# Down-projections of a two-layer kernel: four direct products against seven products of half-size blocks, with block sums made by accumulating DMAs in DRAM

## Reference

```python
FFN_DIM = 2816                      # 22 blocks of 128

def conv_ffn(h, w_up, w_dw, b_dw, w_down):
    u = depthwise_conv(h @ w_up, w_dw) + b_dw      # h (1, 1024, 1024), w_up (1024, 5632), width 3
    gate, val = jnp.split(u, 2, axis=-1)
    return (jax.nn.silu(gate) * val) @ w_down      # (1024, 2816) @ (2816, 1024)

# in each layer, after the token mixer:
h = modulate(rmsnorm(x_lat, g_pre_ffn[i]), m_lat[3], m_lat[4])
x_lat = x_lat + m_lat[5] * rmsnorm(conv_ffn(h, ...), g_post_ffn[i])
```

## Time and profile before

| | us |
|---|---|
| median of 3 runs | 2531.25 (2530.59 to 2535.36) |
| span of the profiled execution, first to last instruction | 2526.5 |
| PE busy in it | 2466.9 (98%) |
| DVE, ACT, POOL busy | 1870.6, 1237.6, 916.5 |

### The profile page before, as it was taken

The page is one execution under the profiler, slowest core; times in us unless marked ns, Lnnn a source line. Parts: engine busy times, 40 slices in busy tenths (PEclk is TensorE's granted clock), DMA queues, the critical chain, the costliest instruction groups (busy, mean ns, idle before and its releaser), DMA issues.

```text
span 2526.5 us, 31835 instructions
## 1 busy us (share of the span) xinstructions
PE 2466.9 (98%) x11292; PEld 1989.2 (79%) x11292; DVE 1870.6 (74%) x2445; ACT 1237.6 (49%) x1998; POOL 916.5 (36%) x611
## 2 busy tenths in 40 slices
PE   8989999999899999999999999999999999999998
PEld 3878888888688788888888877757887888888886
DVE  4467676767458999999437379997689999994352
ACT  3356665666444555555435342236545555554331
POOL 0067486861044566653002100000445656630001
PEclk9999999999999999999999999999999999999999
DMA  6033243330521222222635321020212222236361
GB/s 265 27 109 113 84 133 100 125 100 26 196 100 59 84 88 81 83 88 96 229 130 175 113 80 34 34 67 34 100 59 84 85 82 84 83 101 225 125 207 69
DMA packets 102000, 262.48 MB, mean 104 GB/s; under 512 B 11104, under 2 KB 12384, under 8 KB 101856
## 3 DMA queue, kind: packets, MB, share of 16 engines
q1 hardware_dynamic: 88752, 213.85, 24.8%
q0 software_dynamic: 11520, 41.95, 5.2%
q10 hardware_dynamic: 1584, 4.85, 0.6%
HBM read 216.56 MB, written 44.04 MB: 103 GB/s over the span
## 4 chain that ended last, share of the span: by engine, by line
PE 79%; DVE 15%; issue 2%; ACT 1%; DMA 1%; POOL 0%; SPq 0%; DVEq 0%; POOLq 0%; ACTq 0%
PE psum L2146 23%; PE psum L2148 23%; PE psum L2147 23%; DVE acts L2056 3%; DVE acts L2058 3%; PE psum L2362 3%; PE psum L2351 1%; PE psum L2352 1%; DVE weights_f32r L1753 1%; DVE acts L2060 1%; DVE small L1655 1%; PE psum L2179 1%; DMA low<-x_t 1%; DVE high_f32r L1874 1%; PE psum L2447 1%
## 5 line engine op out<-in xcount | busy, mean ns | idle before, releaser
L2146 PE MATMUL psum<-acts_f32r,weights_f32r 128*128 128x512 f32 x1728 | 683.8, 396 | 8.6 <-DVE acts_f32r L1520 3.0
L2148 PE MATMUL psum<-acts_f32r,weights_f32r 128*128 128x512 f32 x1728 | 674.1, 390 | 0.0
L2147 PE MATMUL psum<-acts_f32r,weights_f32r 128*128 128x512 f32 x1728 | 673.8, 390 | 0.0
L803 POOL TENSOR_TENSOR low<-low 128x512 f32<-128x512 f32 x91 | 132.1, 1452 | 965.4 <-ACT low L1125 960.5
L886 ACT ACTIVATE weights_f32r<-low 128x512 fp32r<-128x512 f32 (+2 forms) x501 | 325.3, 659 | 319.4 <-PE psum L2148 244.5
L2146 PEld LDWEIGHTS psum<-acts_f32r,weights_f32r 128*128 128x128 f32 x1728 | 325.3, 188 | 79.8 <-issue 5.6
L1886 DVE TENSOR_TENSOR weights_f32r<-low,weights_f32r 128x512 fp32r<-128x512 f32 x264 | 379.5, 1482 | 0.1
L2148 PEld LDWEIGHTS psum<-acts_f32r,weights_f32r 128*128 128x128 f32 x1728 | 325.0, 188 | 68.8
L2147 PEld LDWEIGHTS psum<-acts_f32r,weights_f32r 128*128 128x128 f32 x1728 | 325.3, 188 | 68.2 <-issue 2.4
L1893 DVE TENSOR_TENSOR weights_f32r<-low,weights_f32r 128x512 fp32r<-128x512 f32 x176 | 125.6, 719 | 233.9 <-ACT weights_f32r L886 231.0
L830 POOL TENSOR_TENSOR low<-low 128x512 f32<-128x512 f32 x150 | 265.7, 1772 | 39.8 <-DVE acts_f32r L1871 29.3
(11 more groups left out here) (248 smaller groups left out, 4665.7 us busy)
## 6 DMA issues: line engine op xcount, KB each, us to landing
low<-units SPq DMA_DIRECT2D x130, 512.0 KB, 4.0
low<-units SPq DMA_DIRECT2D x176, 256.0 KB, 3.4
set<-mod_w POOLq DMA_DIRECT2D x80, 512.0 KB, 3.9
gated<-low SPq DMA_DIRECT2D x44, 512.0 KB, 2.6
low<-gated SPq DMA_DIRECT2D x88, 256.0 KB, 3.9
residual<-low SPq DMA_DIRECT2D x48, 256.0 KB, 2.0
acts<-mod_w SPq DMA_DIRECT2D x4, 1024.0 KB, 8.8
low<-x_t SPq DMA_DIRECT2D x4, 1024.0 KB, 17.7
```

The lines of the kernel that those rows point to most:

```text
L803: pool.tensor_tensor(acc, first, ring(n), ADD).then_inc(sq_added, 1)
L2146: pe.matmul(out, wl, xh, start=first, stop=False, skip_group_check=continued)
L2147: pe.matmul(out, wh, xl, start=False, stop=False, skip_group_check=continued)
L2148: return pe.matmul(out, wh, xh, start=False, stop=last, skip_group_check=continued)
```

## The change

The contraction of 22 blocks is cut in two halves of 11 (KB), the output in two halves and the tokens in two halves, and the 2 x 2 block product is made as seven products t = 0 to 6 of 11 steps each (ITEMS = 77 steps of 12 matmuls for each layer, before 88). The sums of weight blocks ("S") and of gated blocks ("T") that they need are built in DRAM by DMAs issued by POOL, some of them accumulating; negated gated half blocks, which those sums need, are made by a new ACT copy (`negated`) and stored by SP. Four of the seven results are not an output alone, and DVE combines them (`down_part`). Each step now loads and splits a weight and a gated half block of its own.

```diff
+KB = FB // 2
+ITEMS = 7 * KB
+DOWN = (("W", 0, "B", 0), ("W", 1, "G", 0), ("S", 1, "T", 2), ("S", 0, "T", 4), ("W", 2, "T", 3), ("S", 3, "T", 1), ("S", 2, "G", 1))
+DOWN_BANKS = (0, 0, 1, 0, 1, 0, 0)
 def dn_slot(i):
-    return (i + 2) % 6
+    return (i + 2) % 8
 # SP
             def store_g(layer, j):
                 sp.wait_ge(g_new, FB * layer + j + 1)
+                g = f((FIRST_T if j < 3 else MAIN_T) + L)
+                if j < KB:
+                    dst, g = t_d[layer][j, 0:4].rearrange("i p n -> p i n"), g[:, 0:HALF].unsqueeze(1).to_broadcast([P, 4, HALF])
+            def store_negated(layer, j):
+                sp.wait_ge(n_new, FB * layer + j + 1)
+                sp.dma_start(t_d[layer][j, 4] if j < KB else n_d[layer][j - KB], f(NEGATED, HALF)).then_inc(n_out, 16)
...
 # POOL
+            def weight_sum(layer, n):
+                m, part = divmod(n, 4)
+                sums, base = s_d[layer][m].rearrange("i p n -> p i n"), U_FFN[layer] + 2 * FB + m
+                wait(pool, summed, weights_summed(layer, n))
+                if part == 0:
+                    pool.dma_start(sums, units[base][:, HALF:L].unsqueeze(1).to_broadcast([P, 4, HALF])).then_inc(summed, 16)
+                if part == 1:
+                    pool.dma_start(sums[:, 0:3], units[base][:, 0:HALF].unsqueeze(1).to_broadcast([P, 3, HALF]),
+                                   accum_op=ADD, max_dma_last_dim=4 * HALF).then_inc(summed, 16)
...
                     if k + 2 < CB:
                         pool.dma_start(part, modw[t + 2, k + 2]).then_inc(mod_in[k % 2], 16)
+                    for n in range(4 * KB * (t * CB + k) // (10 * CB), 4 * KB * (t * CB + k + 1) // (10 * CB)):
+                        weight_sum(0, n)
+            def gated_sum(layer, j):
+                pool.wait_ge(g_out, 16 * (FB * layer + j + 1))
+                pool.wait_ge(n_out, 16 * (FB * layer + j + 1))
+                at, n = max(j - KB, 0), j if j < KB else 2 * j - KB
+                sums = t_d[layer][j % KB].rearrange("i p n -> p i n")
+                pool.wait_ge(summed, gated_summed(layer, n))
+                if j < KB:
+                    pool.dma_start(sums[:, 1:4], t_d[layer][j, 4].unsqueeze(1).to_broadcast([P, 3, HALF]), accum_op=ADD, max_dma_last_dim=4 * HALF).then_inc(summed, 16)
+                else:
+                    pool.dma_start(sums[:, 2:5], g_d[layer][at][:, HALF:L].unsqueeze(1).to_broadcast([P, 3, HALF]),
+                                   accum_op=ADD, max_dma_last_dim=4 * HALF).then_inc(summed, 16)
+                    pool.wait_ge(summed, gated_summed(layer, n + 1))
+                    pool.dma_start(sums[:, 3], n_d[layer][at], accum_op=ADD, max_dma_last_dim=4 * HALF).then_inc(summed, 16)
...
                     pool.tensor_tensor(f(U_V + HALF, HALF), f(S_7, HALF), f(S_5, HALF), ADD).then_inc(c22_new, 1)
+                    gated_sum(layer, p)
+                for j in range(MAIN, FB):
+                    gated_sum(layer, j)
...
             down(1)
+            for n in range(4 * KB):
+                weight_sum(1, n)
             mixer(2)
 # ACT, in the up-projection
                         act.wait_ge(c22_new, m)
+                        negated(p + 1)
                         mid(p + 2, 1, f(U_V))
 # DVE, in the down-projection
+                for i in range(6, ITEMS + 4):
+                    t, j = divmod(i, KB)
+                    if i < ITEMS:
+                        split(i)
+                    if t == 7 and j == 0 and b == 1:
+                        t_start(b, 0)
+                        for k in range(CB + 2):
+                            if k < CB:
+                                t_block(b, 0, k)
+                            if k >= 2:
+                                t_rest(b, 0, k - 2, next_h, C_MOD + MODS)
...
+                    if 63 <= i < 70:
+                        renewed(i - 63)
+                    if j == 3 and t:
+                        for c in range(4):
+                            down_part(t - 1, c)
+                    if (t, j) == (5, 7):
+                        stat_scale()
+                        renew_start(b, 0)
+                    if (t, j) == (6, 3):
+                        renewed(7)
 # PE, ahead of the first matmuls of product t into the bank of output block c (bank_free)
+                    if t == 6:
+                        pe.wait_ge(part_new, 24 * layer + 16 + c + 1)
 # PE, in product t
+                    if (t, step) == (5, 2):
+                        pe.wait_ge(part_new, 24 * layer + 16)
+                        stat_cols(b, 0, "y")
+                    if (t, step) == (5, 4):
+                        stat_spread(RT_POST)
```

More of the change, by code:

```diff
@@ L665, in ffn @@
                     load_up(layer, v)
-                for j in range(2):
-                    store_g(layer, j)
+                store_g(layer, 0)
+                store_negated(layer, 0)
+                store_g(layer, 1)
                 for p in range(MAIN):
@@ new lines, in ffn @@
+                for i in range(4, ITEMS):
+                    t, j = divmod(i, KB)
+                    load_down(layer, i)
+                    if i == 6:
+                        store_negated(layer, FB - 2)
+                    if i == 7:
+                        store_g(layer, FB - 1)
+                    if i == 9:
+                        store_negated(layer, FB - 1)
+                    if t == 1 and j == 4:
+                        sp.wait_ge(mm_done, op_done(layer, MAIN - 1, 6))
+                        sp.wait_ge(x_out, 16 * 16 * b)
+                        load_residual(b, 0)
+                    if t == 6 and 1 <= j < 9:
+                        store_x(b, 0, j - 1)
@@ L1225, in silu, with negated @@
                     act.activation(f(at), f(at), ACT.Silu).then_inc(silu_g, 1)
+                def negated(j):
+                    at = (FIRST_T if j < 3 else MAIN_T) + L + (HALF if j < KB else 0)
+                    act.wait_ge(g_new, j0 + j + 1)
+                    wait(act, n_out, 16 * (j0 + j))
+                    copy(f(NEGATED, HALF), f(at, HALF), -1.0).then_inc(n_new, 1)
                 def combined(t, k):
@@ L2589, in ffn, with down @@
                         group_done(mm)
-                def down(turn, j, c):
-                    i = FB * turn + j
+                def down(t, j, c):
+                    i = KB * t + j
                     if c == 0:
                         pe.wait_ge(w_lo, w0 + 139 + i + 1)
-                        if turn % 2 == 0:
-                            pe.wait_ge(g_lo, 2 * FB * layer + FB * (turn // 2) + j + 1)
-                    return three(bank(2 * c + turn % 2), half_unit(dn_slot(i))[c], [g_at(j, p) for p in range(2)], j == 0, j == FB - 1)
@@ L2632, in ffn @@
                     for c in range(4):
-                        for j in range(FB - 4, FB):
-                            mm = down(turn, j, c)
-                            if c == 3 or j == FB - 1:
+                        for j in range(KB - 4, KB):
+                            mm = down(t, j, c)
+                            if c == 3 or j == KB - 1:
                                 group_done(mm)
```

434 lines of the change are left out of this document (224 added, 210 removed).

## The result

The changed kernel takes **2650.4 us** (median of 4 runs, 2646.2 to 2653.3) against 2530.9 us for the kernel before beside it (4 runs, 2526.5 to 2535.4): ratio 1.0467, 95% interval 1.0446 to 1.0489. It is 4.7% slower. Predicted were 2504 us and a range of 2482 to 2588; the prediction is wrong in sign and range.

A forecast was written before the change was run, and what follows sets the result against it. PE, busy 98% of the span, was taken as the bound. Terms -59.8 + 16.4 + 2 + 8.2 + 5.0 + 0.8 = -27.4 us took the span from 2526.5 to 2499.1; plus 4.75 to the median, 2504 us, range 2482 to 2588.

The forecast's parts named there:

- What goes: Matmul steps of 12 fall from 88 to 77 in each of two layers, removing 59.8 us of PE's work.
- POOL in the up-projection: In pairs 11 to 16 POOL's wait for an accumulating DMA overruns its free time: 8.2 us a layer, +16.4 us.
- L: Landing time of an accumulating DMA POOL waits for in pairs 11 to 18, taken as 6.4 us, bounds 3.9 and 8.8.
- 6G - 36.2: Up-projection cost in us a layer over six rounds, G being POOL's new DMA work, L + 1.0, taken as 7.4.
- Attention: 44 weight-sum DMAs hide in POOL's 20 us free per three vectors; loads queued behind sums cost +2 us.
- The upper bound, 66: Attention's largest cost, 66 us, if each weight sum costs POOL 4 us.
- Module: In layer 1's convolution module 44 sums at 5.9 us each take 260 us, hidden in a 300 us gap: 0.
- The threshold of 6.8 us: In the convolution module the sums stay hidden while their mean time stays under 6.8 us.
- Product 6: PE waits 4.1 us a layer at product 6's start for DVE to read product 5's banks: +8.2 us.
- End of layer 0: DVE's scaling, combinations and first unit split finish after PE ends the last product: +5.0 us, bounds 1 and 9.
- Loads: In the down-projection 22 loads of 256 KB a product, 193 GB/s, four steps in flight, cost nothing.
- slow accumulation: Rival, chance 0.28: accumulating DMAs land in 9 us, closing POOL's gaps in up-projection, attention and module: 2585 us; at 12, well over 2650.

The follow-up runs named there:

- e4: Changed kernel with all accumulating DMAs writing without adding, so both sums are left out; number, shapes, order and waits the same: 2540.8 us, ratio 1.0034.
- e5: e1 with POOL issuing a pair's gated sums one step later, behind the next two weight sums, in its idle stretch: 2563.6 us, ratio 1.0132.
- e8: Changed kernel with e5 (including e1), e2, e6, and weight sums placed so none run beside the output projection's loads: 2483.1 us, ratio 0.9812.
- e1: Changed kernel with the second accumulation of each gated block issued a pair later, same DMAs and bytes: 2593.5 us, ratio 1.0249.
- e7: Changed kernel with the accumulating DMAs of the negated halves moving contiguous pieces of 8 KB instead of 2 KB: 2638.8 us, ratio 1.0423.
- e6: Changed kernel's down-projections reordered: DVE combines product 5 before scaling blocks 5 and 6; SP stores the last gated block later: 2629.9 us, ratio 1.0409.
- e2: Changed kernel with SP issuing the first four pw1 unit loads before its wait for t_lo and the residual load: 2634.1 us, ratio 1.0400.
- e3: Changed kernel with the 88 weight sums four in flight, layer 0's moved out of attention's loop, layer 1's in the convolution module: 2607.3 us, ratio 1.0309.

## Why the prediction was wrong

- **What goes, -59.8.** Right.
- **POOL in the up-projection, +16.4; measured 85.2.** The failed step is the size of L. "I take L = 6.4" extended the growth from 256 to 512 KB loads to 1536 KB. Measured is 11.1: e4 shows 7.0 for a plain copy of that shape, so the extension was short already, and 4.1 more with the addition and its smaller packets. The step's own formula was good: with G, POOL's new DMA work in a round, at 1.25 + 10.0 + 0.6 = 11.8 us (219.3 us of waits over 22), 6G - 36.2 gives 34.6 a layer; pairs 11 to 16 lost 33.6 and 32.5. Two other things fell out of the sum: pairs 17 and 18 (8.1), and DVE's stall beside the issue, which was put at nothing since POOL had time (11.0 in pairs 0 to 10; e5 gave back 30 in all, part of it hidden behind POOL's wait in the kernel after).
- **Attention, +2; measured 35.5.** Sums landed in 7.3 to 8.9 us against the 4.5 or 9.1 until the next, and loads behind them in 4.5 instead of 3.9. POOL waited 31.9 us for the sums and 25.3 us longer than before for the loads behind them; PE waited 17.4 us for POOL; the rest are shorter waits for ACT (L1090, 15.0 us for 8.1) and the lower clock behind all of them. The sum had no term for either. With 12 sums left and no wait for them (e8) nothing is lost. The upper bound, 66, held it.
- **Module, 0; measured 13.7.** The mean of 5.9 us a sum was too small, for the same reason as L: 44 sums took 328.6 us (7.47 each), POOL's first addition of squares stood behind them, and PE came 9.6 us late to the matmul that hangs on it. The threshold of 6.8 us was a little low: in the kernel after, e1 and e7 the sums took 327.9 to 335.0 us and PE was 8.9 to 16.0 us late, 319 us less each time, so up to 7.25 us a sum are hidden.
- **Product 6, +8.2; measured 4.3 + 2.7.** Right, and e6 shows DVE's order as its cause. What no term had is the lower clock behind every gap: of the 35.3 us lost in the down-projections the gaps are 28, the rest are some 45 matmuls behind them, 0.4 to 0.6 us apart.
- **End of layer 0, +5.0; measured 13.3, and 6.7 in the stage behind.** I followed DVE's list and left SP's out: its unit loads had moved behind its wait for t_lo. With them in front (e2) 3.7 remain at that place, not far from the 5.0 that DVE's list gave.
- **Loads, 0; measured 4.35 and 3.5 at the start of the down-projections.** SP's list again: the store of the last gated block stood ahead of the loads.

The rival "slow accumulation" was the mechanism. It gave 2585 at L = 9 and "well over 2650" at 12, and L was 11.1. What misled me was the weight: 0.28, on an extrapolation from loads that read one source and don't go from DRAM to DRAM. Three of the prediction's signs of being wrong are in the trace: a landing over 9 us, PE's waits in attention for POOL's sums, and the first squares of layer 1 behind POOL's 44th sum.

## What to carry over

A DMA whose landing an in-order engine waits for costs its latency, not its bandwidth: wait for it a round later, or keep several independent ones in flight where PE has few loads of its own (e3 shows the cost where it has many). Where a change makes new DMAs, read the queues that issue them as lists, SP's too, and find what stands behind each wait. And before the price of an unseen operation decides the sign, weigh the range by its bounds and not by its middle value.

## What was not expected of the hardware

- An accumulating DMA from DRAM to DRAM of 768 KB lands in 7.3 to 11.1 us, a plain copy of the same shape in 4.5 to 7.0; 8 KB pieces for 2 KB gain 0.7.
- POOL's issue depends on the DMA: 0.58 us for a load of 128 rows, 0.76 for 384 rows copied, 1.24 for 384 added, 0.88 for 96 long rows added. Rows alone don't set it: 96 rows added cost more than 384 copied.
- While POOL issues a DMA and goes on with its own additions, a DVE subtraction in SBUF is stretched: by 0.82 us at one adding issue, 1.72 at two, 0.99 at two plain ones with 64-byte rows (hardly any traffic). The taps of DVE beside the issue were not stretched. Why one is and the other isn't, no run shows.
- Other loads paid for the traffic: 512 KB of units landed in 5.8 us for 4.0, with the plain copies in 4.9.
